# Two networks in one kernel on one core: how the normalised rows reach their transposed form

## The chip, the cores and the metric

The kernel runs on one NeuronCore of a Trainium2 chip, as one launch. The metric is the device time of that launch in microseconds (us); lower is better. All arithmetic that the host does is the layout of the inputs and some constants of the shapes.

## The reference, cut to what matters

Two small networks follow each other on 256 rows of 1024 float32 numbers. The first has two layers (retention, then dilated attention, each followed by a SwiGLU feed-forward network) with LayerNorm behind every part; the second has two layers (a mixed block of attention, convolution and a recurrence, then a block with 16384 small experts) with RMSNorm ahead of every part and one at the end. Only the norms matter here:

```python
def _layer_norm(x, g, b):
    mu = jnp.mean(xf, axis=-1, keepdims=True)
    var = jnp.mean(jnp.square(xf - mu), axis=-1, keepdims=True)
    y = (xf - mu) * lax.rsqrt(var + LN_EPS) * g + b
...
x = _layer_norm(DEEPNORM_ALPHA * x + mix, ln_gain[i, 0], ln_bias[i, 0])
...
def rms_norm(x, g):
    y = xf * lax.rsqrt(jnp.mean(xf * xf, axis=-1, keepdims=True) + EPS)
    return (y * g)
...
h2 = rms_norm(x, norm2_g[l])
```

## The kernel before

Weights come from DRAM as 878 tiles of 128 x 1024 float32 numbers (512 KB) on the SP queue, into four buffers `raw`. ScalarE copies each tile rounded into `wh` (`hi`, L432), VectorE subtracts that from `raw` into `wl` (`lo`, L942), and TensorE multiplies with three passes (high x high, high x low, low x high: L1688 to L1690 in `passes`, or L1729 and L1732 in `tile_sums`). Activations are held the same way, as `xh` and `xl`, features on the partitions and the 256 rows on the free axis. The rows themselves, `xr`, are kept the other way round: two chunks `c` = 0 and 1 of 128 rows on the partitions, 1024 features on the free axis.

Nine norms, `NORMS[0]` to `NORMS[8]`, stand between the stages: 0 to 3 are LayerNorms, 4 to 8 RMSNorms. All but 3 and 8 are "split": their result is turned, so that `xh` and `xl` for the next stage come of it. That makes seven split norms: 0, 1, 2 (LayerNorm) and 4, 5, 6, 7 (RMSNorm). Every engine has its own `norm(k)`, and they are ordered by semaphores alone. For one split norm:

- VectorE adds the sums in PSUM to `xr` (`residual`, L962): chunk 0 whole, chunk 1 in two halves. In a LayerNorm it also writes `zc` = (x - mean) * gain (`centred`, L997).
- ScalarE squares and sums (L495, L498, L501, L504, L507) and takes the root (L509).
- VectorE takes the reciprocal (`scaled`, L1003) and multiplies the 128 x 128 identity with it, row by row, into `by_rstd` (L1005, semaphore `n_by`).
- TensorE turns eight blocks of 128 x 128 for each chunk (`turn`, L1701): a float32 matmul of the block with `by_rstd`, so that the transposition and the scaling by the reciprocal deviation are one operation. Chunk 0 has its eight first, then come six of chunk 1; the last two of chunk 1 stand behind the first two steps of the next weight tile. The source is `zc` in a LayerNorm, `xr` in an RMSNorm.
- ScalarE writes `xh` block by block out of PSUM (L519 with the bias in a LayerNorm, L521 with the gain in an RMSNorm), VectorE writes `xl` behind it (L1053, L1057, semaphore `n_lo`), and TensorE takes step `c` of its next weight tile when `n_lo` has counted block `c`.
- In a LayerNorm VectorE also brings `xr` to its new value (`updated`, L1009) some tiles later. Ahead of its eight `xl` blocks it makes the `wl` of a weight tile (`lo(nxt)`), and behind them the next.

VectorE works in the order in which this is written: in a LayerNorm `scaled(0)`, `centred(1)`, `scaled(1)`, `lo(nxt)`, eight `xl`, `lo(nxt + 1)`; in norm 4 `scaled(0)`, `lo(nxt + 1)`, `scaled(1)`; in norms 5 to 7 `scaled(0)`, the second half of `residual` for chunk 1, `scaled(1)`.

Of the kernel before, what the change touches and what calls it, by code (L numbers as in the profile page):

```python
# [24 lines left out]
ALU = mybir.AluOpType  # L25
AX = mybir.AxisListType.X

P = 128
# [67 lines left out]
def build(nc, stream, x_in, consts, ret_c, att_c, vecs, rg_w, keys, scratch, out):  # L96
    with ExitStack() as ctx:
        def sb(name, cols, dt=F32):
            return ctx.enter_context(nc.sbuf_tensor(name, [P, *cols], dt))

        def sem(name):
            return ctx.enter_context(nc.semaphore(name))
# [3 lines left out]
        xr = sb("xr", [NC_T, D])  # L106
# [21 lines left out]
        def ar(off, *shape):  # L128
            n = int(np.prod(shape))
            v = arena[:, off:off + n]  # L130
            if len(shape) == 2:
                v = v.rearrange("p (a b) -> p a b", a=shape[0])
            elif len(shape) == 3:
                v = v.rearrange("p (a b c) -> p a b c", a=shape[0], b=shape[1])
            elif len(shape) == 4:
                v = v.rearrange("p (a b c d) -> p a b c d", a=shape[0], b=shape[1], c=shape[2])
            return v

        ident, ones = cst[:, C_ID:C_ID + P], cst[:, C_ONE:C_ONE + P]
# [4 lines left out]
        zc, squares = ar(0, NC_T, D), ar(2048, D)  # L144
        ln_rows = ar(3072, 2, D)
        by_rstd, nst = ar(5120, NC_T, P), ar(5376, NC_T, 8)
# [4 lines left out]
        zT = [ps[:, bank, at:at + T] for bank, at in  # L151
              ((0, 0), (1, 0), (2, 0), (3, 0), (6, 0), (7, 0), (0, T), (1, T))]
# [44 lines left out]
        def pick_part(off, *shape):  # L197
# [33 lines left out]
        n_acc0, n_half, n_row, n_mu, n_zc, n_std, n_by, n_turned, n_hi, n_lo, n_up = (  # L231
            sem(f"norm_{s}") for s in "first_chunk second_chunk_half residual mean centred std diagonal turned "
            "hi lo updated".split())
# [32 lines left out]
        NORMS = [("ln", "acc", V_LNG, V_LNB), ("ln", "acc", V_LNG + 8, V_LNB + 8),  # L266
                 ("ln", "acc", V_LNG + 16, V_LNB + 16), ("ln", "acc", V_LNG + 24, V_LNB + 24),
                 ("rms", None, V_N1, None), ("rms", "acc", V_N2, None),
                 ("rms", "acc", V_N1 + 8, None), ("rms", "acc", V_N2 + 8, None),
                 ("rms", "acc", V_FIN, None)]  # L270

        split_before = [8 * sum(j not in (3, 8) for j in range(k)) for k in range(10)]
        ln_before = [sum(m == "ln" for m, *_ in NORMS[:k]) for k in range(10)]
# [652 lines left out]
        def _(dve):  # L926
            V = nc.vector
            steps = [0]

            def link(ins, wait=True):  # L930
                steps[0] = steps[0] + 1
                ins.then_inc(dve_step, 1)
                if wait:
                    dve.wait_ge(dve_step, steps[0])
# [31 lines left out]
            def norm(k, nxt=None, before=0, after=0, first_sum=None):  # L966
                kind, source, gain, bias = NORMS[k]
                ln, split = kind == "ln", k not in (3, 8)
# [31 lines left out]
                def scaled(c):  # L1000

                    dve.wait_ge(n_std, 2 * k + c + 1)
                    link(V.reciprocal(nst[:, c, 4:5], nst[:, c, 3:4]))  # L1003
                    if split:
                        V.tensor_scalar(by_rstd[:, c, :], ident, nst[:, c, 4:5], None, ALU.mult).then_inc(n_by, 1)  # L1005

                def updated(c):

                    V.scalar_tensor_tensor(out=xr[:, c, :], in0=zc[:, c, :], scalar=nst[:, c, 4:5],  # L1009
                                           in1=ln_rows[:, 1, :], op0=ALU.mult, op1=ALU.add).then_inc(n_up, 1)  # L1010

# [7 lines left out]
                if source is None:  # L1019
                    scaled(0)  # L1020
                    lo(nxt + 1)
                    scaled(1)
                else:
                    row0()
                    if ln:
                        centred(0)
                    row1_half()
                    if not ln:
                        scaled(0)
                    if k == 8:  # L1030
                        dve.wait_ge(ln_in, 8 * 16 * 4 + 16)
                        out_piece(*OUT_PIECES[0])
                    row1()
                    if ln:
                        scaled(0)
                    if k == 3:
                        updated(0)
                    if ln:
                        centred(1)
                    scaled(1)  # L1040
                    if ln and split:
                        lo(nxt)
                    if k == 3:
                        updated(1)
                    elif k == 8:
                        for piece in OUT_PIECES[1:]:
                            out_piece(*piece)
# [14 lines left out]
                if ln:  # L1062
                    for n in range(3):
                        lo(nxt + 2 + n)
                        first_sum(n)
                        if n:
                            updated(n - 1)
# [10 lines left out]
            for g in range(4):  # L1078
                dve.wait_ge(x_hi, g + 1)
                b = slice(2 * g, 2 * g + 2)  # L1080
# [28 lines left out]
            for m in range(16):  # L1109
                lo(m + 2)  # L1110
                if m % 4 == 3:
                    h = m // 4
# [193 lines left out]
            for p in range(1, DB):  # L1306
                for i in range(6):
                    lo(g0 + 24 + 6 * p + i + 2)
                    qk_sum(p, i)
                    h = 2 * (p - 1)  # L1310
# [33 lines left out]
            for k in range(2):  # L1344
# [6 lines left out]
                z = [fz[0:H2, j, :] for j in range(6)]  # L1351
# [159 lines left out]
                split = 16 * FULL_ROWS  # L1511
# [170 lines left out]
        def _(pe):  # L1682
            M = nc.tensor.matmul
# [13 lines left out]
                    pe.wait_ge(evac, e - 1 + (0 if i is None else i * ebody))  # L1697

            def turn(k, c, b):
                src = zc if NORMS[k][0] == "ln" else xr  # L1700
                ins = M(zT[b][:, c * P:(c + 1) * P], src[:, c, b * P:(b + 1) * P], by_rstd[:, c, :],  # L1701
                        start=True, stop=True)
                if c == 1:
                    ins.then_inc(n_turned, 1)

# [131 lines left out]
            def norm(k):  # L1837
                kind, source = NORMS[k][0], NORMS[k][1]
                for c in range(NC_T):
                    pe.wait_ge(n_by, split_before[k] // 4 + c + 1)  # L1840
                    if kind == "ln":
                        pe.wait_ge(n_zc, 2 * ln_before[k] + c + 1)
                    for b in (0, 1, 4, 5, 6, 7, 2, 3) if c == 0 else range(6):
                        if (c, b) == (0, 2) and source is not None:
                            pe.wait_ge(n_row, row_before[k] + 3)
                        turn(k, c, b)

            pe.wait_ge(const_in, 16)
            pe.wait_ge(x_in_s, 16)
            for b in range(DB):  # L1850
                for c in range(NC_T):
                    ins = nc.tensor.transpose(acc[:, b, c * P:(c + 1) * P], xr[:, c, b * P:(b + 1) * P], ident)
# [109 lines left out]
            for i in range(6):  # L1962
                tile_sums(g0 + i, e0 + i, norm=1 if i == 0 else None)
                if i == 2:
                    pe.wait_ge(attc_in, 16)
                    for g in range(G3):
                        ins = M(ps_a[0:AH, g, 0:384], ac[0:33, G3 * 384 + g * AH:G3 * 384 + (g + 1) * AH],
                                ac[0:33, g * 384:(g + 1) * 384], start=True, stop=True)
# [118 lines left out]
            for k in range(2):  # L2087
# [143 lines left out]
                for c in range(NC_T):  # L2231
                    for m, src in enumerate((ee[:, 0, :, :], ee[:, 1, :, :], ge)):
                        ins = nc.tensor.transpose(ps_x[:, c, m * P:(m + 1) * P],
                                                  src[:, 8 * c:8 * c + 8, :].rearrange("p h j -> p (h j)"), ident)
# [169 lines left out]
```

## Time and profile before

| | |
|---|---|
| Median of 3 runs | 2810.3 us (2809.2 to 2810.81) |
| The profiled execution | 2811.18 us, its span 2809.4 us |
| TensorE busy, its weight loads | 98%, 88% of the span |
| VectorE, ScalarE busy | 71%, 56% |
| Mean granted TensorE clock | 0.995 |

A row of the timeline gives start, duration, engine, line, operation, output and inputs, shape and count; in square brackets stands the idle time of the engine ahead of it and what ended it. A float32 matmul of `turn` leaves two records (two passes), a transposition one. Durations of neighbours on one engine overlap, since each includes its own way in and out; what an operation costs its queue is the distance from its start to the next start.

### The profile page before, as it was taken

What the parts mean: (1) busy time and instruction counts of PE and PEld (TensorE: products, weight loads), DVE (VectorE), ACT (ScalarE), POOL (GpSimd) and SP (SyncE); (2) the same over time, 40 slices, a digit from 0 to 9 for tenths busy, and PEclk for the clock granted to TensorE, in tenths of its full rate; (3) what the DMA queues carried; (4) which work ended last, traced back from release to release, by engine and by line L of the source; (5) the groups of instructions that cost most, each with busy time, mean ns of one, the idle gap of its engine ahead of it and who ended that gap; (6) DMA issues with size and microseconds to landing.
All of it is one profiled execution on the core that took longest, in us unless ns stands there. A gap on an engine that the chain in (4) does not pass through costs nothing.

```text
span 2809.4 us, 49471 instructions
## 1 busy us (share of the span) xinstructions
PE 2756.2 (98%) x17443; PEld 2472.6 (88%) x17443; DVE 2004.6 (71%) x3314; ACT 1568.7 (56%) x2759; POOL 32.2 (1%) x63
## 2 busy tenths in 40 slices
PE   8999999999999999999999999998999999999998
PEld 7888888887887889999998888887999999988887
DVE  6767675676766869977886555577799678855555
ACT  4355454555545665557775555575555677645454
POOL 0000000000000000000000000000000000000000
PEclk9999999999999999999999999999999999999999
DMA  6445656554554345554445555553455444465554
GB/s 214 156 152 181 196 179 203 179 177 143 182 197 156 133 147 176 180 179 141 138 143 173 193 194 193 191 173 114 157 181 185 159 143 137 146 199 193 194 194 165
DMA packets 164944, 480.20 MB, mean 171 GB/s; under 512 B 15840, under 2 KB 58848, under 8 KB 164672
## 3 DMA queue, kind: packets, MB, share of 16 engines
q1 hardware_dynamic: 161424, 467.72, 50.3%
q0 software_dynamic: 3232, 10.20, 1.1%
q8 instruction: 93, 1.52, 0.2%
q14 instruction: 51, 0.42, 0.1%
q10 hardware_dynamic: 144, 0.34, 0.0%
HBM read 477.02 MB, written 1.18 MB: 170 GB/s over the span
## 4 chain that ended last, share of the span: by engine, by line
PE 91%; DVE 5%; ACT 2%; DMA 1%; issue 1%; DVEq 0%; ACTq 0%; POOLq 0%
PE ps L1688 22%; PE ps L1689 22%; PE ps L1690 22%; PE ps L1729 10%; PE ps L1732 5%; PE ps L2248 4%; DVE wl L942 1%; DMA raw<-stream_dram 1%; PE ps L1701 1%; ACT wh L432 1%; DVE arena L1383 1%; DVE xr L962 1%; PE ps L2214 1%; PE ps L1987 0%; PE ps L2030 0%
## 5 line engine op out<-in xcount | busy, mean ns | idle before, releaser
L942 DVE TENSOR_TENSOR wl<-raw,wh 128x1024 fp32r<-128x1024 f32 x878 | 1074.1, 1224 | 569.2 <-ACT wh L432 561.5
L432 ACT ACTIVATE wh<-raw 128x1024 fp32r<-128x1024 f32 x878 | 928.2, 1058 | 493.7 <-DMA raw<-stream_dram 485.1
L1688 PE MATMUL ps<-xs,wh 128*128 128x256 f32 x2576 | 743.7, 289 | 0.3 <-DVE wl L942 0.2
L1689 PE MATMUL ps<-xs,wh 128*128 128x256 f32 x2576 | 729.6, 283 | 0.0
L1690 PE MATMUL ps<-xs,wl 128*128 128x256 f32 x2576 | 729.3, 283 | 0.0
L1688 PE MATMUL ps<-wh,mh 128*128 128x512 f32 x1304 | 509.4, 391 | 2.0 <-DVE wl L942 1.1
L1690 PE MATMUL ps<-wh,ml 128*128 128x512 f32 x1304 | 507.4, 389 | 0.0
L1689 PE MATMUL ps<-wl,mh 128*128 128x512 f32 x1304 | 507.4, 389 | 0.0
L1688 PEld LDWEIGHTS ps<-xs,wh 128*128 128x128 f32 x2576 | 495.0, 192 | 0.8 <-DVE wl L942 0.4
L1689 PEld LDWEIGHTS ps<-xs,wh 128*128 128x128 f32 x2576 | 495.3, 192 | 0.1
L1690 PEld LDWEIGHTS ps<-xs,wl 128*128 128x128 f32 x2576 | 494.5, 192 | 0.0
L1729 PE MATMUL ps<-xs,wh 128*128 128x512 f32 x1344 | 441.4, 400 | 2.1 <-DVE arena L948 1.0
L1732 PEld LDWEIGHTS ps<-xs,wl 128*128 128x128 f32 x1344 | 252.6, 188 | 56.9
L1688 PEld LDWEIGHTS ps<-wh,mh 128*128 128x128 f32 x1304 | 244.8, 188 | 54.9 <-DVE wl L942 4.0
L1690 PEld LDWEIGHTS ps<-wh,ml 128*128 128x128 f32 x1304 | 244.8, 188 | 51.0
L1689 PEld LDWEIGHTS ps<-wl,mh 128*128 128x128 f32 x1304 | 244.8, 188 | 50.5
L1732 PE MATMUL ps<-xs,wl 128*128 128x256 f32 x1344 | 265.2, 278 | 0.0
L1729 PEld LDWEIGHTS ps<-xs,wh 128*128 128x128 f32 x1344 | 210.8, 189 | 10.8 <-issue 7.0
L446 ACT ACTIVATE arena<-ps 128x256 f32 (+1 forms) x188 | 72.0, 384 | 215.1 <-PE ps L1690 214.6
L483 ACT ACTIVATE mh<-arena 128x512 fp32r (+1 forms) x158 | 99.5, 630 | 89.2 <-PE ps L1690 80.2
L954 DVE TENSOR_TENSOR ml<-arena,mh 128x512 fp32r<-128x512 f32 x158 | 108.7, 689 | 46.6 <-ACT mh L483 46.3
L1644 DVE TENSOR_TENSOR arena<-arena,ps 128x252 f32<-128x252 f32 (+42 forms) x128 | 70.2, 549 | 93.4 <-ACT arena L892 93.4
(300 smaller groups left out, 2552.0 us busy)
## 6 DMA issues: line engine op xcount, KB each, us to landing
raw<-stream_dram SPq DMA_DIRECT2D x878, 512.0 KB, 3.3
arena<-norm_rows POOLq DMA_DIRECT2D x32, 128.0 KB, 3.6
picks<-bias_scratch SPq DMA_DIRECT2D x24, 128.0 KB, 3.6
arena<-bias_scratch SPq DMA_DIRECT2D x24, 128.0 KB, 3.6
arena<-keys_dram POOLq DMA_DIRECT2D x16, 128.0 KB, 3.4
arena<-ret_c_dram POOLq DMA_DIRECT2D x1, 1344.0 KB, 5.9
xr<-x_dram POOLq DMA_DIRECT2D x1, 1024.0 KB, 7.9
arena<-rg_w_dram POOLq DMA_DIRECT2D x4, 128.0 KB, 3.2
```

The lines of the kernel that those rows point to most:

```text
L432: A(wh[b % 4][:, :, :], raw[:, b % 4, :].rearrange("p (a b) -> p a b", a=DB), ACT.Copy) \
L446: A(dst, src, func, scale=scale, **kw).then_inc(evac, 1)
L483: A(mh[:, s:s + 2, :], src, ACT.Copy).then_inc(m_hi, 1)
L942: V.tensor_tensor(wl[b % 4][:, :, :], raw[:, b % 4, :].rearrange("p (a b) -> p a b", a=DB), wh[b % 4][:, :, :].bitcast(F32), ALU.subtract) ...
L954: V.tensor_tensor(ml[:, s:s + 2, :], src, mh[:, s:s + 2, :].bitcast(F32), ALU.subtract) \
L1644: V.tensor_tensor(h, h, ps_a[:, n % 4, :].rearrange("p (t m) -> p m t", t=4)[:, 0:known, :], ALU.mult).then_inc(g_mul, 1)
L1688: M(out_ap, lh, rh, start=first, stop=False, skip_group_check=skip)
L1689: M(out_ap, lh, rl, start=False, stop=False, skip_group_check=skip)
L1690: return M(out_ap, ll, rh, start=False, stop=last, skip_group_check=skip)
L1729: ins = M(bank, wh[b % 4][:, c, :], xs[:, c, :, :].rearrange("p a t -> p (a t)"), start=(c == 0), stop=(c == DB - 1), skip_group_check=True)
L1732: ins = M(bank[:, 0:T], wl[b % 4][:, c, :], xh[:, c, :], start=False, stop=False, skip_group_check=True)
L2248: ins = M(ps_a[:, n % 4, j * P:(j + 1) * P], gated[n % 3][:, j, :], oh[n % 2][:, 4 + j, :].bitcast(F32), start=True, stop=True)
```

## The change

In `scaled` VectorE multiplies 512 columns of the rows at a time by the reciprocal deviation, twice for each chunk, into `zc`, in place of the 128 x 128 identity. `turn` then is a plain transposition by the constant identity. Chunk 0 of the LayerNorms is left as it was: the identity is scaled, and a matmul turns. The turns of blocks 4 and on wait for the second piece. `updated(1)` of a split LayerNorm has scaled rows before it, so it only adds the bias. In an RMSNorm `turn` now reads `zc`, not `xr`. `n_by` counts four for each split norm, not two.

```diff
--- before.py
+++ after.py
@@ -1001,11 +1001,24 @@
 
                     dve.wait_ge(n_std, 2 * k + c + 1)
                     link(V.reciprocal(nst[:, c, 4:5], nst[:, c, 3:4]))
-                    if split:
-                        V.tensor_scalar(by_rstd[:, c, :], ident, nst[:, c, 4:5], None, ALU.mult).then_inc(n_by, 1)
+                    if not split:
+                        return
+                    if ln and c == 0:
+                        V.tensor_scalar(by_rstd[:, c, :], ident, nst[:, c, 4:5], None, ALU.mult).then_inc(n_by, 2)
+                        return
+                    if ln:
+                        dve.wait_ge(n_zc, 2 * ln_before[k] + c + 1)
+                    for h in range(2):
+                        a, z = 512 * h, 512 * (h + 1)
+                        src = zc[:, c, a:z] if ln else xr[:, c, a:z]
+                        V.tensor_scalar(zc[:, c, a:z], src, nst[:, c, 4:5], None, ALU.mult).then_inc(n_by, 1)
 
                 def updated(c):
 
+                    if split and c == 1:
+                        dve.wait_ge(n_by, split_before[k] // 2 + 4)
+                        V.tensor_tensor(xr[:, c, :], zc[:, c, :], ln_rows[:, 1, :], ALU.add).then_inc(n_up, 1)
+                        return
                     V.scalar_tensor_tensor(out=xr[:, c, :], in0=zc[:, c, :], scalar=nst[:, c, 4:5],
                                            in1=ln_rows[:, 1, :], op0=ALU.mult, op1=ALU.add).then_inc(n_up, 1)
 
@@ -1697,9 +1710,11 @@
                     pe.wait_ge(evac, e - 1 + (0 if i is None else i * ebody))
 
             def turn(k, c, b):
-                src = zc if NORMS[k][0] == "ln" else xr
-                ins = M(zT[b][:, c * P:(c + 1) * P], src[:, c, b * P:(b + 1) * P], by_rstd[:, c, :],
-                        start=True, stop=True)
+                dst, src = zT[b][:, c * P:(c + 1) * P], zc[:, c, b * P:(b + 1) * P]
+                if NORMS[k][0] == "ln" and c == 0:
+                    ins = M(dst, src, by_rstd[:, c, :], start=True, stop=True)
+                else:
+                    ins = nc.tensor.transpose(dst, src, ident)
                 if c == 1:
                     ins.then_inc(n_turned, 1)
 
@@ -1837,12 +1852,14 @@
             def norm(k):
                 kind, source = NORMS[k][0], NORMS[k][1]
                 for c in range(NC_T):
-                    pe.wait_ge(n_by, split_before[k] // 4 + c + 1)
+                    pe.wait_ge(n_by, split_before[k] // 2 + 2 * c + 1)
                     if kind == "ln":
                         pe.wait_ge(n_zc, 2 * ln_before[k] + c + 1)
                     for b in (0, 1, 4, 5, 6, 7, 2, 3) if c == 0 else range(6):
                         if (c, b) == (0, 2) and source is not None:
                             pe.wait_ge(n_row, row_before[k] + 3)
+                        if b == 4:
+                            pe.wait_ge(n_by, split_before[k] // 2 + 2 * c + 2)
                         turn(k, c, b)
 
             pe.wait_ge(const_in, 16)
```

## Rows read from the trace of the kernel before

**Rows 1.** The page: busy time of each engine, and the chain's shares.

```profile
PE 2756.2 (98%) x17443; PEld 2472.6 (88%) x17443; DVE 2004.6 (71%) x3314; ACT 1568.7 (56%) x2759; POOL 32.2 (1%) x63
...
PE 91%; DVE 5%; ACT 2%; DMA 1%; issue 1%; DVEq 0%; ACTq 0%; POOLq 0%
```

**Rows 2.** Chain that ended last, norm 0: start us, us, what.

```profile
226.31 0.28 DVE arena L1005
226.60 1.14 DVE wl L942
...
227.74 3.23 DVE xs L1053 x8
230.97 1.14 DVE wl L942
...
232.16 0.50 PE ps L1729
```

**Rows 3.** Timeline, norm 0: turns, then ScalarE's `xh` blocks.

```profile
224.92 3.39 PE L1701 MATMUL ps<-arena 128*128 128x128 f32 x28 [1.43 <-DVE arena L1005]
...
227.24 3.03 ACT L519 ACTIVATE xs<-ps,vec 128x256 fp32r<-128x256 f32 x8 [0.20 <-PE ps L1701]
```

**Rows 4.** VectorE's groups by form: count | busy us, mean ns | idle.

```profile
L1269 DVE TENSOR_SCALAR arena<-arena 128x768 f32<-128x768 f32 x16 | 9.9, 621 | 0.6
...
L1269 DVE TENSOR_SCALAR arena<-arena 128x256 f32<-128x256 f32 x16 | 5.6, 353 | 0.6
...
L1005 DVE TENSOR_SCALAR arena<-cst,arena 128x128 f32<-128x128 f32 x14 | 4.0, 286 | 0.5
...
L1117 DVE TENSOR_SCALAR arena<-ps,arena 128x512 f32<-128x512 f32 x4 | 3.0, 752 | 0.1
```

**Rows 5.** Timeline, transpositions elsewhere: of the start, and of the expert stage.

```profile
9.35 3.65 PE L1852 MATMUL ps<-cst,xr 128*128 128x128 f32 x16 [9.35 <-DMA xr<-x_dram]
...
13.86 0.41 PE L1690 MATMUL ps<-wh,xs 128*128 128x512 f32 x1
...
1247.31 0.82 PE L2233 MATMUL ps<-cst,picks 128*128 128x128 f32 x6
```

**Rows 6.** Timeline, norm 4: second `by_rstd`, `xh`, next weight tile.

```profile
897.93 0.29 DVE L1005 TENSOR_SCALAR arena<-cst,arena 128x128 f32<-128x128 f32 x1
900.88 3.09 ACT L521 ACTIVATE xs<-ps,vec 128x256 fp32r<-128x256 f32 x8 [3.18 <-PE ps L1701]
...
902.02 0.36 PE L1688 MATMUL ps<-xs,wh 128*128 128x256 f32 x1
```

**Rows 7.** Timeline, norm 5: turns, second `by_rstd`, `xh`, next weight tile.

```profile
1014.78 6.26 PE L1701 MATMUL ps<-arena,xr 128*128 128x128 f32 x28 [2.89 <-DVE arena L1005]
...
1016.69 0.29 DVE L1005 TENSOR_SCALAR arena<-cst,arena 128x128 f32<-128x128 f32 x1
1019.02 3.69 ACT L521 ACTIVATE xs<-ps,vec 128x256 fp32r<-128x256 f32 x8 [2.57 <-PE ps L1701]
...
1020.77 0.39 PE L1688 MATMUL ps<-xs,wh 128*128 128x256 f32 x1
```

**Rows 8.** Timeline, norm 6: turns of chunk 1, second weight tile.

```profile
1851.45 1.60 PE L1701 MATMUL ps<-arena,xr 128*128 128x128 f32 x12 [0.21 <-DVE arena L1005]
...
1856.89 0.39 PE L1688 MATMUL ps<-xs,wh 128*128 128x256 f32 x1 [0.24 <-DVE wl L942]
```

**Rows 9.** Windows: from:to length, busy us by engine, granted clock, DMA, GB/s.

```profile
894.60:901.30 6.70, 4.66 (x22) 4.66 (x23) 3.50 (x8) 3.45 (x8) 0.00 (x0) 0.50 0.14 58
...
1014.10:1020.80 6.70, 6.02 (x29) 6.03 (x29) 2.76 (x8) 3.80 (x12) 0.00 (x0) 0.50 0.26 103
...
952.60:955.90 3.30, 3.30 (x18) 3.30 (x16) 3.23 (x8) 1.54 (x3) 0.00 (x0) 0.50 0.03 5
...
1966.40:1973.10 6.70, 4.69 (x22) 4.69 (x23) 2.02 (x6) 3.77 (x11) 0.00 (x0) 0.50 0.19 74
```

**Rows 10.** Timeline, norm 7: first pass of the next weight tile.

```profile
1973.80 0.36 PE L1688 MATMUL ps<-xs,wh 128*128 128x256 f32 x1
```

## The prediction

> **What bounds the kernel now.** I read the page first. TensorE is busy 98% of the span and makes 91% of the chain that ended last; VectorE makes 5% of it [rows 1]. So almost everywhere only TensorE's work counts. But the change touches seven short stretches, and there I read the chain and the timeline instead of the shares.
>
> In the LayerNorms 0 to 2 (norm 0 stands for all three) the chain runs through VectorE without a break: the scaled identity of chunk 1 at 226.31, a `wl` tile from 226.60, eight `xl` blocks from 227.74, another `wl` tile from 230.97, and only then TensorE's second weight tile at 232.16 [rows 2]. TensorE's turns are done well inside that, and ScalarE, which needs 3.03 us for its eight `xh` blocks, starts at 227.24 and is ahead of VectorE all the way [rows 3].
>
> In the RMSNorms 4, 5 and 7 the order is the other way. In norm 5 the identity of chunk 1 is ready at about 1016.98, but the first `xh` block starts only at 1019.02, because TensorE is still turning chunk 0: its 28 records take 6.26 us [rows 7]. The granted clock tells why. It is 0.50 from 1014.1 to 1020.8, that is 1.2 GHz of 2.4, after TensorE had stood idle [rows 9]; behind that a pass of the weight tile takes its warm 0.39 us [rows 7]. Norms 4 and 7 look the same (0.50 from 894.6 to 901.3 and from 1966.4 to 1973.1) [rows 9]. Norm 6 is warm: 12 records of its chunk 1 take 1.60 us, and TensorE's wait at 1856.89 is for VectorE's `wl` [rows 8]. There the path is VectorE's and ScalarE's, as in a LayerNorm.
>
> **The cost of a turn.** Warm, 28 records in 3.39 us are 0.12 us for a record, 0.23 to 0.24 for a turn of two [rows 3]. A transposition elsewhere leaves one record: six in 0.82 us, whose last record includes some 0.27 us of its own way, so 0.11 each [rows 5]. At the low clock it is 0.46 for a turn (norm 5: 14 turns in 6.26 less the tail [rows 7]) against about 0.21 for a transposition (16 in 3.65 less the tail of 0.42 [rows 5]). So a turn is halved, by 0.12 us warm and 0.25 us cold. The 16 turns of a norm save TensorE some 2 us at the high and 4 us at the low clock (half of it in a LayerNorm), if TensorE is what is waited for.
>
> **The cost of a piece.** No row has 512 columns multiplied by a column out of SBUF. Rows with 256 and 768 columns take 353 and 621 ns, 0.52 ns a column, so 512 take 0.49 us; about 0.08 of that overlaps the next instruction, so a piece costs VectorE's queue 0.41 us and two cost 0.82 [rows 4]. The identity took 286 ns, less the same overlap 0.20 us [rows 4]. Two pieces in place of it: +0.62 us. Upper bound for a piece: 752 ns, the 512 columns out of PSUM (L1117) [rows 4]. Lower bound: the 353 ns of 256 columns, less 0.08. The source and the output are both in SBUF as in the rows of 256 and 768, so I take those.
>
> **LayerNorms 0, 1, 2.** Chunk 0 is unchanged. In `scaled(1)` the +0.62 stands on the chain: behind it are `lo(nxt)`, all eight `xl` and the next `lo`, and TensorE's second tile waits for the last of them [rows 2]. The first piece is ready at 226.31 + 0.49 = 226.80, when chunk 0's turns end anyway, so ScalarE starts where it did, and its head start covers the rest. The cheaper turns of chunk 1 are covered by VectorE and give nothing. `updated(1)` has one multiplication less, of no price here. Sum: 3 x 0.62 = +1.8 us, of which I count 1.7, since a little of such lateness is caught up in idle VectorE time.
>
> **Norm 4.** Two pieces and `lo` stand ahead of the second reciprocal, so the first piece of chunk 1 starts at 897.93 + 0.61 = 898.54 and ends at 899.03. Chunk 0's transpositions have ended by then (896.84 + 8 x 0.21 = 898.5). One cold transposition and the usual 0.1 later ScalarE starts at 899.4, in place of 900.88; TensorE's tile follows by 1.14 as in the rows, at 900.5 in place of 902.02 [rows 6]. That is -1.5, and two cheaper turns inside the tile give another -0.2. Against it stands the clock. Before, TensorE began turning at 896.6, and the clock rose 4.7 us later, ahead of the tile; in norm 5 it rose 6.0 us after the turns began [rows 7, 9]. Now the tile begins 3.7 us after the turns did, so it runs its first 1.0 to 2.3 us at half speed, which costs 0.5 to 1.15. If the 6 us count from the end of the new gap between the two chunks, the tile is cold for 4.6 us and it costs 2.2 or more. Norm 4: -1.2 to +0.5; I take -0.6.
>
> **Norms 5 and 7.** The pieces of chunk 0 push the second half of `residual` by 0.62, and with it the square, the root and the reciprocal of chunk 1: its first piece starts at 1016.69 + 0.62 = 1017.31 and ends at 1017.80. With a cold transposition and 0.1, ScalarE starts at 1018.1 to 1018.2, in place of 1019.02, and the tile at 1019.3, in place of 1020.7 [rows 7]. The gain is 1.4 + 0.2. But chunk 0 is turned by 1016.8, so TensorE now stands idle for 1 us in the middle of the turns, and the clock has to rise while the tile runs. At 4.7 to 6.0 us from 1015.0 it rises at 1019.7 to 1021.0, cost 0.2 to 0.85; at 6.0 us from the end of the gap, at 1023.9, cost 2.3. Norm 5: -1.4 to +0.7. Norm 7 had its clock back by 1973.1, ahead of its tile at 1973.8 [rows 9, 10], so its tile comes 0.8 us earlier, not 1.4: -0.85 to +1.25. Since the gap falls in the very time in which the clock used to come back, I take the upper half: +0.4 and +0.5.
>
> **Norm 6.** Warm before. Its VectorE path gets +0.62 for `residual`, +0.20 for the longer first piece, and -0.12 for the transposition: +0.7 on the tile at 1856.89 [rows 8]. TensorE has only 1.7 us of transpositions between the stages now, spread over 5 us with gaps of 0.9 and 1.6. The clock may fall, as it does elsewhere; the shortest cold stretch that the windows show is 3.3 us (952.6 to 955.9, 0.50) [rows 9], and such a stretch over the tile costs 1.7, a double one over 2. Norm 6: +0.7 to +2.9; I take +1.5, as I hold a fall for somewhat likelier than not.
>
> **Sum.** 1.7 - 0.6 + 0.4 + 0.5 + 1.5 = +3.5 us on the profiled execution of 2811.18 us, 2814.7; that execution stands 0.9 above the median of the runs, so for the median 2810.3 + 3.5 = 2813.8 us. With the lower ends: 1.7 - 1.2 - 1.4 - 0.85 + 0.7 = -1.1, so 2809.2. With the upper ones: 1.7 + 0.5 + 0.7 + 1.25 + 2.9 = +7.1, so 2817.4. DMA is not touched: the loads follow `mm_done`, and the bias and gain rows are loaded tiles later.
>
> **A rule that speaks against the change.** First the row: at the start of the kernel TensorE does 16 transpositions from 9.35 to about 12.8 and hardly anything else, and the pass at 13.86 already takes 0.41 us, its warm time [rows 5]. So transpositions brought the clock up there. The Trainium skill, "TensorE: Matmul & The Clock Gate", Part 4, says that the full clock does not engage for transpose mode, since it doesn't count as TensorE being busy in the same way. By that rule the low stretches would begin in the LayerNorms too and last longer in all others, a result of some +9 us where the row gives +3.5 (rival 1 has the price). The trace disagrees with it as far as the start of the kernel shows, where a few ordinary passes stood behind the transpositions.
>
> **Rivals.**
> 1. The low clock spreads. In each of the LayerNorms TensorE idles 1.43 us ahead of the turns today and stays warm [rows 3]. Now it turns chunk 1 in 0.7 us and idles again for over 1 us until the first `xl`. If that makes the clock fall, a cold stretch of 3.3 us costs 1.7 in each of three norms (+5), and norms 4 to 7 take their upper ends. With 5 us for the first, 2810.3 + 3.5 + 5 = 2818.8; with all of it, 2810.3 + 7.1 + 5 = 2822.4. It decides from one fall on. For it: halved work, more gaps. Against it: chunk 0 keeps its matmuls there, and transpositions brought the clock up at the start [rows 5]. Chance 0.2. The rule of the Trainium skill quoted above leads here.
> 2. TensorE's half price wins: the clock comes back as early as before despite the gaps, and norm 6 stays warm. Then the lower ends hold, 2809.2 us; if in addition the idle VectorE time behind the LayerNorms takes up the 1.7, 2807.5 us. It decides where the clock rises within 6.0 us of the first turn in norms 5 and 7. Chance 0.17.
> 3. The pieces run at the single rate of L1117, 0.68 us of queue for each [rows 4]. That adds 0.54 to each LayerNorm and about 0.54 + 0.27 to each of norms 4 to 7: 1.6 + 3.2, so 2813.8 + 4.8 = 2818.6 us. Against it: the straight line of the SBUF rows. Chance 0.05.
>
> **How the numbers follow.** The forecast, a small loss of 1 to 6 us, has 0.58. A measurement of this kernel can tell about 0.2%, 5.6 us, from no change. Over 2815.9 lie rival 1, nearly whole, most of rival 3 and a small part of the forecast: 0.24. Under 2804.7 nothing that I can work out ends; 0.03 is left for it. Within 0.2%: 0.73. The range has to take in the lower ends and most of rival 1: 2808.0 to 2819.0.
>
> **What would show it.** In the profile after: L1005 gone from the RMSNorms, and new rows of 128x512 at about 490 ns; turns of one record each, 0.11 us warm; in norm 0 the second weight tile 0.6 us later behind the first `residual` than before; in norm 5 `xh` starting 3.7 us behind the first piece and not 4.6; the granted clock low for longer in norms 5 and 7, and possibly low in norm 6. It would be wrong if the clock stays down in the LayerNorms, or if pieces take 0.75 us.

## The result and the profile after

The changed kernel takes 2813.84 us, the median of 20 runs, against 2809.26 us of the kernel before, also 20 runs: a ratio of 1.0014, with a 95% interval of 1.0008 to 1.002, so +2.2 to +5.6 us with +4.6 as the difference of the medians. The change costs a little, below the 0.2% that I had called measurable, though twenty runs of each do set it apart from nothing. The profiled execution took 2812.22 us, with a span of 2810.4.

The page after, to be read beside [rows 1]:

```profile
span 2810.4 us, 49312 instructions
...
PE 2751.7 (98%) x17355; PEld 2464.6 (88%) x17355; DVE 2013.2 (72%) x3325; ACT 1571.9 (56%) x2759; POOL 32.2 (1%) x63
...
PE 91%; DVE 5%; ACT 2%; issue 1%; DMA 1%; DVEq 0%; ACTq 0%; SPq 0%; POOLq 0%
```

TensorE has fewer records (17355 for 17443) and 4.5 us less work. VectorE has 8.6 us more. Neither sum says what the change costs; that is read at the seven norms.

The new operations, VectorE's groups by form (count | busy us, mean ns | idle before):

```profile
L1014 DVE TENSOR_SCALAR arena<-xr,arena 128x512 f32<-128x512 f32 x16 | 7.1, 483 | 0.3
...
L1020 DVE TENSOR_TENSOR xr<-arena 128x1024 f32<-128x1024 f32 x3 | 3.6, 1214 | 0.0
...
L1014 DVE TENSOR_SCALAR arena<-arena 128x512 f32<-128x512 f32 x6 | 2.6, 484 | 0.1
L1007 DVE TENSOR_SCALAR arena<-cst,arena 128x128 f32<-128x128 f32 x3 | 0.9, 286 | 0.3
```

A piece takes 483 ns, where the line through the rows of [rows 4] gave 490. The identity is left only at L1007, three times.

**Norm 0.** The chain that ended last in the kernel after (start us, us, what), which answers to [rows 2]:

```profile
220.54 1.24 DVE xr L962 x2
...
226.74 0.88 DVE arena L1014 x2
227.62 1.13 DVE wl L942
228.76 3.14 DVE xs L1066 x8
231.89 1.14 DVE wl L942
233.04 0.04 issue
233.08 0.50 PE ps L1744
```

and the start of the same chain in the kernel before:

```profile
220.14 1.24 DVE xr L962 x2
```

The two executions stand 0.4 us apart here, so I count from the first `residual` (L962). The `wl` tile behind the pieces starts 7.08 us behind it, before 6.46: the +0.62 of the forecast, exactly. The second weight tile starts 12.54 us behind it, before 12.02: +0.52. The 0.1 came back inside the eight `xl` blocks, which take 3.14 us and not 3.23.

The timeline of the same norm shows TensorE and ScalarE, beside [rows 3]:

```profile
225.42 2.05 PE L1715 MATMUL ps<-arena 128*128 128x128 f32 x16 [1.50 <-DVE arena L1007]
...
227.31 0.85 PE L1717 MATMUL ps<-cst,arena 128*128 128x128 f32 x6
227.65 3.32 ACT L519 ACTIVATE xs<-ps,vec 128x256 fp32r<-128x256 f32 x8 [0.19 <-PE ps L1717]
```

Chunk 1's six transpositions take 0.85 us, where twelve records of matmuls stood. It gains nothing: ScalarE waits 0.19 us for the first block, before 0.20. `xh` starts 7.11 us behind `residual`, before 7.10.

**Norms 4 to 6.** The timeline of norm 4, of norm 5 and of norm 6, in that order, beside [rows 6 to 8]:

```profile
899.03 1.97 PE L1717 MATMUL ps<-cst,arena 128*128 128x128 f32 x8 [6.06 <-DVE arena L1014]
901.16 1.54 PE L1717 MATMUL ps<-cst,arena 128*128 128x128 f32 x6 [0.16 <-DVE arena L1014]
901.67 3.04 ACT L521 ACTIVATE xs<-ps,vec 128x256 fp32r<-128x256 f32 x8 [1.78 <-PE ps L1717]
...
1014.94 0.88 DVE L1014 TENSOR_SCALAR arena<-xr,arena 128x512 f32<-128x512 f32 x2
1015.48 1.97 PE L1717 MATMUL ps<-cst,arena 128*128 128x128 f32 x8 [3.02 <-DVE arena L1014]
1017.79 0.88 DVE L1014 TENSOR_SCALAR arena<-xr,arena 128x512 f32<-128x512 f32 x2
1018.33 1.54 PE L1717 MATMUL ps<-cst,arena 128*128 128x128 f32 x6 [0.89 <-DVE arena L1014]
1018.84 2.85 ACT L521 ACTIVATE xs<-ps,vec 128x256 fp32r<-128x256 f32 x7 [1.28 <-PE ps L1717]
1019.98 0.55 PE L1701 MATMUL ps<-xs,wh 128*128 128x256 f32 x1
...
1849.36 1.43 PE L1717 MATMUL ps<-cst,arena 128*128 128x128 f32 x8 [0.86 <-DVE arena L1014]
1852.21 1.54 PE L1717 MATMUL ps<-cst,arena 128*128 128x128 f32 x6 [1.42 <-DVE arena L1014]
1852.72 2.85 ACT L521 ACTIVATE xs<-ps,vec 128x256 fp32r<-128x256 f32 x7 [0.34 <-PE ps L1717]
```

In norm 5 `xh` starts 3.90 us behind the first piece, and the tile at 1019.98, 1.14 later. But the pass there takes 0.55 us in place of 0.39 [rows 7], and TensorE has a new hole of 0.89 us between the chunks. In norm 6, once warm [rows 8], the six transpositions of chunk 1 take 1.54 us, as in norm 5, where norm 0 has 0.85. The windows say why (columns as in [rows 9]; norms 4, 5, 6, 7):

```profile
895.95:902.70 6.75, 3.51 (x14) 2.61 (x14) 5.96 (x12) 4.90 (x12) 0.00 (x0) 0.50 0.21 77
1015.50:1022.20 6.70, 5.71 (x24) 4.83 (x25) 4.81 (x12) 4.08 (x12) 0.00 (x0) 0.50 0.17 68
1851.70:1858.40 6.70, 6.08 (x27) 5.71 (x28) 5.65 (x14) 4.88 (x10) 0.00 (x0) 0.50 0.17 71
1967.80:1977.90 10.10, 8.22 (x36) 7.35 (x37) 7.20 (x16) 6.23 (x16) 0.00 (x0) 0.50 0.20 78
```

The clock is at 0.50 (1.2 GHz of 2.4) in norm 6 too, for 6.7 us, and in norm 7 for 10.1 us and not 6.7. In norms 5, 6 and 7 the tile runs on it. The stretch behind norm 4 (952.6 before, 954.0 after) is there in both.

**The whole, norm by norm.** To put a size on each norm I counted in each trace TensorE's records from the next weight tile's first pass on, without those of the turns, and took the time from the norm's first `residual` to the record behind six tiles' worth of them (6 x 16 in a LayerNorm, 6 x 24 in an RMSNorm). I call it the seventh tile. In norms 0 and 2 it is indeed the first pass of that tile. In norms 1, 4 and 6 it is the first of some small matmuls that stand 1.0 to 1.6 us ahead of it, and in norms 5 and 7, where small matmuls stand earlier, a pass 1.9 us ahead of it. It is the same record in every kernel, so the differences hold. By then tiles follow each other in their old rhythm, 2.8 or 2.9 us apart. Each kernel was profiled a second time (`before_again`, `after_again`), since two executions of one kernel differ in where the clock falls. us:

| norm | before, twice | after, twice | change of the mean |
|---|---|---|---|
| 0 | 26.51, 26.52 | 26.97, 26.94 | +0.44 |
| 1 | 27.26, 27.27 | 27.78, 27.76 | +0.50 |
| 2 | 26.44, 28.05 | 26.86, 26.87 | -0.38 |
| 4 | 31.86, 32.07 | 30.23, 31.10 | -1.30 |
| 5 | 26.97, 25.82 | 26.44, 27.59 | +0.62 |
| 6 | 25.50, 25.49 | 27.63, 26.77 | +1.70 |
| 7 | 26.34, 26.01 | 27.54, 27.26 | +1.22 |
| sum | 190.88, 191.23 | 193.45, 194.29 | +2.8 |

In norm 2 one execution of before had a low clock; against the other the change is +0.42, and the sum +3.6.

The rest of the span, outside these seven stretches, is 2618.5 and 2617.8 us before and 2617.0 and 2613.7 after. So the four spans (2809.4 and 2809.0, 2810.4 and 2808.0) have the same mean, and the local loss can't be seen in them: what differs between executions elsewhere is larger. The loss of the whole kernel rests on the twenty timed runs, its places on the norms.

### The profile page after: what moved, and what is told of

It is laid out like the page before. It is cut to its first block, busy times and chain, and to the rows that moved or that the text cites. A ratio compares the mean times of both kernels' runs of the same rounds, so it can differ in the third digit from the quotient of the medians.

```text
span 2810.4 us, 49312 instructions
## 1 busy us (share of the span) xinstructions
PE 2751.7 (98%) x17355; PEld 2464.6 (88%) x17355; DVE 2013.2 (72%) x3325; ACT 1571.9 (56%) x2759; POOL 32.2 (1%) x63
## 4 chain that ended last, share of the span: by engine, by line
PE 91%; DVE 5%; ACT 2%; issue 1%; DMA 1%; DVEq 0%; ACTq 0%; SPq 0%; POOLq 0%
PE ps L1701 22%; PE ps L1702 22%; PE ps L1703 22%; PE ps L1744 10%; PE ps L1747 5%; PE ps L2265 4%; DVE wl L942 1%; DMA raw<-stream_dram 1%; ACT wh L432 1%; DVE arena L1396 1%; DVE xr L962 1%; PE ps L2231 1%; PE ps L2004 0%; PE ps L2047 0%; DVE arena L997 0%
```

## The experiments

Each ratio is to the kernel before, timed beside the variant; behind it stands its 95% interval. "Seventh tile" is the measure of the table above. Each variant has one profiled execution, so a norm's value carries the scatter that the two executions of one kernel show there.

**Which part costs: `ln_part`, `rms_part`.** The first changes only the LayerNorms, the second only norms 4 to 7.

```diff
# ln_part, on after: scaled(), turn()
-                    if ln and c == 0:
+                    if not ln or c == 0:
...
-                dst, src = zT[b][:, c * P:(c + 1) * P], zc[:, c, b * P:(b + 1) * P]
-                if NORMS[k][0] == "ln" and c == 0:
+                ln = NORMS[k][0] == "ln"
+                dst, src = zT[b][:, c * P:(c + 1) * P], (zc if ln else xr)[:, c, b * P:(b + 1) * P]
+                if not ln or c == 0:
# rms_part, on after: scaled(), updated(), turn()
-                    if ln and c == 0:
+                    if ln:
...
-                    if split and c == 1:
+                    if False:
...
-                if NORMS[k][0] == "ln" and c == 0:
+                if ln:
```

> Only norms 0 to 2 are changed, the RMSNorms are as before. Two theories. Queue theory (mine): the two pieces in place of the scaled identity stand in VectorE's queue on the chain, +0.60 us for each LayerNorm, so +1.8 us on the kernel before; in the profile the second weight tile behind each LayerNorm comes 0.6 us later, and the clock is as before. Clock theory (rival): such lateness is caught up, the whole loss of the change comes of the low TensorE clock at the RMSNorms, and this kernel is within 0.5 us of the one before.

> Only norms 4 to 7 are changed, the LayerNorms are as before. Queue theory with the clock's part as forecast: +1.8 to +2.8 us. Clock theory: the whole +4.6 us. A third way, that the clock costs nothing and only pieces and cheaper turns count: -2.8 us (the lower ends of the forecast). In the profile I expect a low stretch of the clock at norm 6 in some executions, and longer ones at 5 and 7.

Measured: `ln_part` 2809.39 us against 2810.78, ratio 0.9996 (0.9987 to 1.0005); `rms_part` 2812.01 us, 1.0009 (1.0 to 1.0018). For `ln_part` the interval is -3.7 to +1.4 us: my +1.8 lies outside it, and the rival's 0 inside. For `rms_part` it is 0 to +5.1, which rules out the -2.8 but can't tell +1.8 from +4.6. So by the whole times the LayerNorms seem to cost nothing. The traces say otherwise: in `ln_part` the seventh tile is at 26.96 and 27.78 in norms 0 and 1 (+0.45 and +0.5, as in after), and norms 4 to 7 (32.41, 25.82, 25.64, 26.09) are within 0.4 us of an execution of before. In `rms_part` norms 0 to 2 are within 0.2 of before, and norms 6 and 7 at 27.65 and 27.56, as in after. Norm by norm each part looks as it does in after, so I see no sign that they act on each other; the whole times are too wide to show it. The LayerNorms' +1.4 in the traces is not confirmed by the time of `ln_part`. Its profiled execution has a cold stretch in norm 2 (27.96), as `before_again` has (28.05); at that norm, once cold, the pieces show no cost.

**VectorE's pieces or TensorE's transpositions: `pieces_matmul`.** VectorE does all of its new work, and TensorE turns by float32 matmuls with the unscaled identity, two records for a turn.

```diff
-                    ins = nc.tensor.transpose(dst, src, ident)
+                    ins = M(dst, src, ident, start=True, stop=True)
```

> VectorE's pieces as in the change, but TensorE turns them by a float32 matmul with the identity, two passes as before. LayerNorms +1.8 us by the queue theory (TensorE is covered there), 0 by the clock theory. RMSNorms: TensorE is as busy as before, so the clock should behave as before; norm 6 +0.8, the others +0.2 each for the longer first piece: +1.4. Queue theory +3.2 us, clock theory +1.4 us. If the plain transposition itself is what costs, this kernel is clearly better than the changed one.

Measured: 2812.16 us, 1.0006 (0.9997 to 1.0015). The timeline of norm 5:

```profile
1019.57 4.75 PE L1717 MATMUL ps<-cst,arena 128*128 128x128 f32 x28 [3.00 <-DVE arena L1014]
...
1023.24 3.04 ACT L521 ACTIVATE xs<-ps,vec 128x256 fp32r<-128x256 f32 x8 [1.59 <-PE ps L1717]
```

The interval, -0.8 to +4.2 us, holds both forecasts (+3.2 and +1.4). The 28 records bridge the hole between the chunks. The low clock here lasted from 1019.0 to 1022.4, 3.4 us and not 6.7, though `before_again` has 3.4 us there too. Norm 6 had none, and norm 7 had 3.4 us, where after has 10.2 and 6.8. The seventh tile is at 25.94, 26.29 and 26.22 in norms 5, 6 and 7, where the two executions of after have means of 27.02, 27.20 and 27.40. So with the same VectorE work, the full work on TensorE keeps the clock in norm 6 and shortens the low stretch in norm 7, and that is worth some 0.9 and 1.2 us. In norm 4 the transpositions win: 32.38 with matmuls against 30.23 and 31.10. Norms 0 and 1 stay at 26.96 and 27.76: their loss is VectorE's alone. (Norm 2 was cold here, 27.74.)

The timed runs say the same of the clock, without a trace. The mean granted clock is 0.9954 in the 33 runs of before beside these variants, 0.9956 in `ln_part` and 0.9954 in `pieces_matmul`, but 0.9930 in `rms_part` and 0.9927 in the 20 runs of after. So the added low clock comes with the transpositions of the RMSNorms, and not with the pieces.

**Does VectorE's lateness reach the end: `double_pieces`.** Each piece of a LayerNorm has an extra multiply of 512 columns ahead of it, whose result nothing reads.

```diff
                         a, z = 512 * h, 512 * (h + 1)
+                        if ln:
+                            V.tensor_scalar(ar(5632, 512) if h else picks[:, 1536:2048], cst[:, 0:512],
+                                            nst[:, c, 4:5], None, ALU.mult)
                         src = zc[:, c, a:z] if ln else xr[:, c, a:z]
```

> The changed kernel, with one more multiplication of 512 columns into unused memory ahead of each piece of a LayerNorm: 0.80 us more in VectorE's queue for each of three LayerNorms. Queue theory: +2.4 us on top of the change, so +7.0 us on the kernel before. Clock theory (lateness is caught up): the same as the change, +4.6 us.

Measured: 2815.7 us against 2810.78, 1.0017 (1.0008 to 1.0026). The chain of norm 0:

```profile
226.97 0.49 DVE picks L1014
227.46 0.40 DVE arena L1017
227.86 0.40 DVE arena L1014
228.25 0.40 DVE arena L1017
```

Four multiplies take 1.68 us of the chain, two took 0.88 in after: +0.80. The seventh tile comes at 27.74, 28.56 and 27.66 in the three LayerNorms, +0.77, +0.78 and +0.80 over after. Lateness of VectorE there passes on in full as far as the seventh tile. Whether it reaches the end, the whole time can't decide: its interval, +2.2 to +7.3 us over before, holds both +7.0 and +4.6.

**The low clock taken away: `before_filled`, `after_filled`.** TensorE does float32 matmuls of 256 columns, whose result nothing reads, while it would idle ahead of the turns of norms 4 to 7; in after also between the chunks.

```diff
                 for c in range(NC_T):
+                    for _ in range({4: 24, 5: 12, 6: 2, 7: 14}.get(k, 0) if c == 0 else 0):
+                        M(ps[:, 7, T:], ident, cst[:, 0:T], start=True, stop=True)
```

(in `after_filled` 4 of them for c == 1 in norms 5, 6 and 7)

> The kernel before, with idle work for TensorE (float32 matmuls of constants, 0.23 us each warm, into a free half of a PSUM bank) in the time in which it stands idle ahead of the turns of norms 4 to 7: 24, 12, 2 and 14 of them. By my account of the clock it then does not fall there: no low stretch at norms 4, 5 and 7, the turns at their warm 0.24 us, the xh blocks 2.3 us sooner in norm 4 and 1.3 to 1.7 us sooner in norms 5 and 7, and 4 to 5 us less than the kernel before in all. If the low clock costs nothing there (VectorE and ScalarE would set the time anyway), no difference.

> The changed kernel with the same idle work, and four more of these matmuls between the turns of the two chunks in norms 5 to 7. With the clock up on both sides only VectorE's queue is left of the change. Queue theory: +0.5 us in each LayerNorm and +0.7 us in each of norms 4 to 7 on the filled kernel before, so about +4.3 us on that and within 1 us of the kernel before. If cheaper turns are a gain of their own once the clock is up, this kernel is as fast as the filled one before or faster.

Measured: 2812.42 us against 2809.14, 1.0016 (1.0007 to 1.0025), and 2814.32, 1.0021 (1.0012 to 1.003): no gain, where I had expected 4 to 5 us. `after_filled` is 1.9 us above `before_filled` by the medians, not 4.3. I had sized the fills wrongly, so this pair says little of the change. The timeline of `before_filled` at norm 4 and at norm 5, each a part of the fill:

```profile
890.49 9.87 PE L1841 MATMUL ps<-cst 128*128 128x256 f32 x45
...
1013.94 2.32 PE L1841 MATMUL ps<-cst 128*128 128x256 f32 x10
```

Ten records in 2.32 us are 0.23 each. The first row is cut at the end of the stretch that I asked for; in all the 24 matmuls of norm 4 left 48 records in 10.52 us, two for each matmul. So one takes 0.45 us and not 0.23. The fill overran the idle time: in norm 4 the first turn came 12.91 us behind `residual` (before 8.69), in norm 7 6.25 (before 3.30), and the seventh tiles there are late with them (34.04 and 27.24). Norm 5, where it fitted better (first turn at 3.66), shows what it was for: 24.86 to the seventh tile, in place of 26.97 and 25.82.

**Finer filling, and the rule on transpositions: `before_filled_tr`.** Idle transpositions in their place.

```diff
+                    for _ in range({4: 48, 5: 24, 6: 4, 7: 28}.get(k, 0) if c == 0 else 0):
+                        nc.tensor.transpose(ps[:, 7, T:T + P], flip, ident)
```

> As the filled kernel before, but the idle work is plain transpositions (48, 24, 4 and 28, 0.11 us each warm). If transpositions keep TensorE's clock up as matmuls do, which the start of the kernel before suggests, no low stretch at norms 4, 5 and 7 and 4 to 5 us less than the kernel before. By the rule of the Trainium skill (TensorE: Matmul & The Clock Gate, Part 4: transpose mode doesn't count as busy in the same way) the clock falls as in the kernel before, and so does nothing for the time: 0.

Measured: 2806.01 us, 0.9991 (0.9982 to 1.0), which is 0 to 5 us less. The mean granted clock of its timed runs is 0.9978, against 0.9957 of before beside it. Its timeline at norm 5 and at norm 7, and its window behind the start of norm 5's turns:

```profile
1009.39 2.78 PE L1841 MATMUL ps<-cst 128*128 128x128 f32 x24
1014.19 5.02 PE L1701 MATMUL ps<-arena,xr 128*128 128x128 f32 x28 [2.02 <-DVE arena L1005]
...
1963.72 3.22 PE L1841 MATMUL ps<-cst 128*128 128x128 f32 x28
1969.03 1.60 PE L1701 MATMUL ps<-arena,xr 128*128 128x128 f32 x12 [0.20 <-DVE arena L1005]
```

```profile
1014.70:1018.10 3.40, 3.40 (x18) 3.40 (x18) 0.48 (x3) 1.16 (x4) 0.00 (x0) 0.51 0.00 1
```

At norm 5 the fill ended 2.02 us before the turns, and the clock was low for 3.4 us. At norm 7 it stayed up: chunk 1's twelve records in 1.60 us, the seventh tile at 24.86 in place of 26.34 and 26.01. Norm 4 was warm as well, at 29.93 in place of 31.86 and 32.07.

**Both kernels without the low clock: `before_kept`, `after_kept`.** The counts set so that the fill ends close to the turns, and put into the LayerNorms too.

```diff
+                    for _ in range({0: 12, 1: 12, 2: 20, 4: 50, 5: 34, 6: 5, 7: 34}[k] if c == 0 else 0):
+                        nc.tensor.transpose(ps[:, 7, T:T + P], flip, ident)
# after_kept, for c == 1: {0: 0, 1: 0, 2: 0, 4: 4, 5: 9, 6: 12, 7: 9}[k]
```

> The kernel before with idle transpositions ahead of the turns of all seven split norms: 12, 12, 20 at norms 0, 1, 2 and 50, 34, 5, 34 at norms 4 to 7. The first filled kernel with transpositions left a low stretch at norm 5, where TensorE stood idle for 2 us behind them; the longer filling should take it away: seventh weight tile behind norm 5 at 24.9 us after the residual (26.97 and 25.82 in two executions before), norm 4 at 29.9, norm 7 at 24.9, norm 2 always at 26.4, not 28.05. In all 3 to 5 us less than the kernel before, which would make it the fastest here.

> The changed kernel with the same filling, and 4, 9, 12 and 9 idle transpositions between the two chunks in norms 4 to 7. With the clock up in both, what is left of the change is VectorE's queue: +0.5 us in each LayerNorm, +0.6 to 0.8 us in each of norms 4 to 7, so about +4.3 us on the kept kernel before. If the cheaper turns are worth something by themselves, the difference is smaller, in norm 4 above all.

Measured: `before_kept` 2803.72 us against 2810.73, 0.9976 (0.9966 to 0.9986), the fastest of all, 7.0 us under the kernel before where I had forecast 3 to 5. `after_kept` 2808.07 us, 0.9993 (0.9984 to 1.0002), 4.35 us over `before_kept`, as forecast (+4.3). The page of `before_kept`, its timeline of norm 4, its windows at norms 4 to 7, and last the window of `after_kept` at norm 6:

```profile
span 2800.1 us, 49805 instructions
...
PE 2765.9 (99%) x17610; PEld 2482.8 (89%) x17610; DVE 2007.7 (72%) x3314; ACT 1564.3 (56%) x2759; POOL 32.3 (1%) x63
```

```profile
891.31 5.62 PE L1841 MATMUL ps<-cst 128*128 128x128 f32 x50
897.49 3.39 PE L1701 MATMUL ps<-arena,xr 128*128 128x128 f32 x28 [0.55 <-DVE arena L1005]
899.80 3.04 ACT L521 ACTIVATE xs<-ps,vec 128x256 fp32r<-128x256 f32 x8 [1.25 <-PE ps L1701]
```

```profile
889.00:899.00 10.00, 9.45 (x74) 8.73 (x73) 9.67 (x19) 7.03 (x15) 0.00 (x0) 1.00 0.44 159
1006.00:1016.00 10.00, 10.00 (x77) 9.33 (x75) 4.99 (x11) 6.86 (x15) 0.00 (x0) 1.00 0.28 105
1842.00:1850.00 8.00, 7.71 (x56) 6.75 (x55) 4.72 (x13) 7.10 (x18) 0.00 (x0) 1.00 0.58 197
1956.00:1966.00 10.00, 9.94 (x78) 9.30 (x77) 5.54 (x11) 7.39 (x17) 0.00 (x0) 1.00 0.28 105
...
1846.00:1858.00 12.00, 10.22 (x73) 8.60 (x73) 9.24 (x22) 9.68 (x21) 0.54 (x1) 1.00 0.42 138
```

TensorE does 9.7 us more work than before and the span is 9.3 us shorter. The 28 records of the turns take 3.39 us in norm 4, as warm in [rows 3]. The seventh tiles:

| norm | 0 | 1 | 2 | 4 | 5 | 6 | 7 | sum |
|---|---|---|---|---|---|---|---|---|
| `before_kept` | 26.52 | 27.28 | 26.43 | 29.92 | 25.01 | 25.50 | 25.08 | 185.74 |
| `after_kept` | 26.95 | 27.78 | 26.87 | 30.08 | 25.28 | 26.14 | 25.28 | 188.38 |

In norms 5 and 7 the fill of `before_kept` ran on too long: the first turn came 4.02 and 4.08 us behind `residual`, unfilled 3.3. In norm 7 of `after_kept` it came at 4.14, unfilled 3.5. The fills of the LayerNorms changed nothing. Part of the 7.0 us lies elsewhere: the seven norms hold 5.3 of it, 4.5 without the cold norm 2 of before, and the low stretch behind norm 4 is gone in `before_kept` and `after_kept`, as it is in `after_again`.

**The second profiles: `before_again`, `after_again`.** One execution each:

> The kernel before once more, for a second profile of it: how far the low stretches of the clock and the times from the first residual to the seventh weight tile behind each norm differ between two executions of one kernel. I expect the LayerNorms within 0.1 us, norms 5 and 7 within 1 us, norm 6 warm again.

> The changed kernel once more, for a second profile. By my account: LayerNorms 0.5 us later than before, norm 4 gaining 0.5 to 1.9 us, norm 5 between 26.4 and 26.6 us, norm 6 at 27.6 us with a low stretch, norm 7 at 26.1 to 27.6 us.

Measured: 2810.82 and 2809.79 us. Their rows are in the first table. Of before I had expected norms 5 and 7 within 1 us of each other; norm 5 differs by 1.15. Of after I had norm 5 at 26.4 to 26.6 (27.59) and norm 6 at 27.6 (26.77): where the clock falls can't be foretold to the microsecond. `before_again` has a stretch in norm 2 that `before` does not have; its window, and its turns there:

```profile
702.20:705.40 3.20, 3.20 (x15) 3.20 (x16) 2.68 (x4) 2.03 (x4) 0.00 (x0) 0.50 0.64 255
```

```profile
702.15 4.54 PE L1701 MATMUL ps<-arena 128*128 128x128 f32 x24 [2.03 <-DVE arena L1005]
```

## Why the prediction was right, point by point

The forecast was 2813.8 us and a small loss for the named reasons; 2813.84 was measured. That the two agree to a tenth is luck: the interval of the difference is 3.4 us wide, the forecast started from 2810.3, 1.0 above the kernel before as timed beside the change, and its +3.5 is 1.1 below the measured +4.6. In the steps too, errors of norms 4 and 7 cancel. The steps:

- **The piece** (0.49 us, 0.41 of queue): 0.48 and 0.40 to 0.44. Right, and rival 3 (single rate, 0.75 us) is out.
- **The LayerNorms** (+0.62 each on the chain, 1.7 counted in all): the +0.62 is there at the `wl` tile, and +0.42 to +0.52 reaches the seventh tile, 1.4 us in all. `double_pieces` shows that such lateness passes through in full; of what came back, 0.1 is inside the `xl` blocks of norm 0, and where the rest goes no row here shows. By the traces the term was 0.3 too large; the time of `ln_part` would have it smaller still.
- **Norm 4** (-0.6, between -1.2 and +0.5): -1.3 on the mean of two, just beyond the lower end. The tile came 1.4 us earlier as worked out (12.67 us behind `residual`, before 14.07; -1.5 forecast), and the clock, low from 895.9 to 902.7, was back 3.7 us behind the first turn, just ahead of the tile at 902.81 (901.67 and 1.14), where I had reckoned with 4.7 or more. So in this execution the charge of 0.5 to 1.15 us for a cold tile did not fall due, and norm 4 gained 1.7. In `after_again` the clock was back only 5.7 us behind the first turn, the tile ran its first 1.9 us cold, and norm 4 gained 0.9. The mechanism is as forecast in both; the term was mis-sized by 0.7.
- **Norm 5** (+0.4): the tile came 1.29 us earlier than in `before` (-1.4 forecast), though only 0.19 earlier than in `before_again`, whose low stretch was the shorter. It ran 2.2 us of its time cold; +0.6 on the means of two that lie 1.2 apart. The clock was back 6.7 and 9.4 us behind the first turn, beyond the 4.7 to 6.0 of the rows, as the upper half of the range supposed. **Norm 7** (+0.5): +1.2, near the upper end of +1.25, with a stretch of 10.2 us in one execution and 6.8 in the other. It was mis-sized by 0.7 too, the other way than norm 4. That the new hole between the chunks is the place fits `pieces_matmul`, which has no such hole and 3.4 us of low clock in each; but `before_again` has 3.4 in each as well, so it is likely and not shown.
- **Norm 6** (+1.5, between +0.7 and +2.9): +2.13 and +1.28, with 6.8 and 3.4 us of low clock where there was none. That the clock may fall in a norm that was warm is confirmed in both executions, and in `rms_part` and `double_pieces`; with matmuls there (before twice, `ln_part`, `pieces_matmul`) it never did.
- **The sum** (+3.5): locally +2.8 on the means, +3.6 without the one cold norm 2 of before, and +4.6 (2.2 to 5.6) in the whole times. Whether something outside the norms adds to it stays open: the kept pair differs by 2.6 us in the norms and by 4.35 in the medians, and the interval of each of its ratios reaches 2.5 to 2.8 us to either side.

**How the loss divides.** With the clock kept up, the change costs 188.38 - 185.74 = 2.6 us in the norms: 1.4 in the LayerNorms and 1.3 in norms 4 to 7. There `xh` starts 0.4 to 0.6 us later than with warm matmuls. Some of that comes back inside the first tile, whose two turns are cheaper: in norm 4 the tile starts 0.38 us later and the second one 0.16, in norm 5 0.49 and 0.27. In norm 6, where the second tile waits for VectorE's `wl`, it is 0.64 and 0.64. So once the clock is up the halved turns give back some 0.2 us in each of norms 4, 5 and 7, less than the pieces cost. The 2.6 is rather low: the fill that ran on too long left norms 5 and 7 of `before_kept` at 25.01 and 25.08, where `before_filled` and `before_filled_tr` have 24.86.

With the clock as it falls, `pieces_matmul` divides the loss. Put norm 2 at its warm value and its sum is 192.4, against 190.3 for before and 193.9 for after (means of two): +2.2 for the pieces and +1.4 more for the transpositions, which gain in norm 4 and lose in norms 5 to 7. The low clock costs before (190.88 + 191.23)/2 - 185.74 = 5.3 us in the norms, or 4.5 without its cold norm 2, and after (193.45 + 194.29)/2 - 188.38 = 5.5. The change moves this cost from norm 4 to norms 6 and 7 and adds up to 1 us to it. The forecast had 1.7 for the LayerNorms' pieces and +1.8 for the rest as a balance of gain and clock. That balance was right in kind: the pieces are the larger part of the loss, and the clock the smaller. These are sums of one or two executions, so each is good to about 1 us.

**The rivals.** Rival 1 (the low clock spreads to the LayerNorms) did not happen: norms 0 to 2 of both executions of after are warm. The only norm of these that fell is norm 2, in `before_again`, `ln_part` and `after_filled` and in `pieces_matmul`, so in changed and unchanged kernels alike. Rival 2 (half price wins) held in norm 4 and failed in norms 5 to 7: its mark was a clock back within 6.0 us of the first turn in norms 5 and 7, and it took 6.7 to 9.4 us. Rival 3 is out by the 483 ns. The rule of the Trainium skill, "TensorE: Matmul & The Clock Gate", Part 4, that transpose mode does not bring the full clock, is not borne out: in `before_kept` 50 transpositions in a row, 0.11 us each, stand ahead of norm 4's turns, where TensorE idled before, and the granted clock is 1.00. Norm 6 of `after_kept` is the cleanest case: turns and fill are all transpositions there, from 1847.6 to 1853.3, and its window has 1.00, while the same turns without fill fell to 0.50 in both executions of after. So in these rows it is the idle time and not the kind of work that brings the clock down. How well transpositions alone raise a clock that is down, no run here shows: at the start of the kernel, on which the prediction leant, the first pass behind the 16 transpositions, at 12.86, still took 0.78 us, and two passes later it was 0.41.

## What to carry to other kernels

When a step feeds an engine that is 98% busy, a cheaper instruction there is worth nothing unless that engine is the one waited for at that spot; price the work put on the other engine first: where that engine stands on the chain its lateness went through in full here. Before shortening TensorE's work between two waits, read the granted clock there: shorter work leaves more idle time, and that may cost what it saves; above all don't expect a norm that is warm today to stay so. Where a low clock stands behind a known idle time, cheap transpositions that nothing reads, ending just before the real work, gave 7 us here (0.9976), more than the change under study could move.

## What the runs showed of the hardware

- An idle float32 transposition of 128 x 128 takes 0.11 us warm (50 in 5.62 us) and keeps the granted clock at 1.00.
- A float32 matmul is two records of its column count each: 0.45 us for 256 columns, twice what I had allowed.
- The same kernel falls to the low clock at different norms, and for different times, from one execution to the next: norm 2 in one of two of before, norm 7 for 10.2 or 6.8 us in after. A fall is worth 1 to 1.6 us, so one profile can't settle a question of that size.
- With the fill stopped 2.02 us ahead of the turns the clock fell in norm 5 of `before_filled_tr`; with 0.65 us in its norm 4 and 0.55 us in `before_kept` it did not. The idle time alone does not settle it: norm 2 of before idles 2.03 us ahead of its turns in both executions, and fell in one.
